# Operands of the dense products at different places modulo 2048 bytes

## The reference, cut to what matters

```python
# first block, each layer
h = rms_norm(x, pre_gain) * (1.0 + scale) + shift
proj = h @ w_in                       # then attention, retention, gated linear attention
y = jnp.concatenate([a_out, r_out, g_out], axis=-1) @ w_out
x = x + gate * rms_norm(y, post_gain)

# second block, each layer: mixers (window attention, spatial gating, fourier), then
def squared_relu_mlp(h, w1, w2):      # w1 is 1024 x 4096, w2 4096 x 1024
    return jnp.square(jax.nn.relu(h @ w1)) @ w2
```

## Time and profile before

| | |
|---|---|
| median of 3 runs | 3961.57 us |
| profiled execution, its own time | 3959.07 us |
| its span | 3957.3 us |
| mean granted TensorE clock | 0.976 of full speed |
| TensorE busy, matmul | 3674.5 us (93% of the span) |
| VectorE, ScalarE, GpSimd busy | 2127.4, 1725.4, 1775.3 us |
| DMA, mean | 106 GB/s |

### The profile page before, as it was taken

The page is one execution under the profiler, slowest core; times in us unless marked ns, Lnnn a source line. Parts: engine busy times, 40 slices in busy tenths (PEclk is TensorE's granted clock), DMA queues, the critical chain, the costliest instruction groups (busy, mean ns, idle before and its releaser), DMA issues.

```text
span 3957.3 us, 61376 instructions
## 1 busy us (share of the span) xinstructions
PE 3674.5 (93%) x22388; PEld 2983.7 (75%) x22388; DVE 2127.4 (54%) x3355; ACT 1725.4 (44%) x2899; POOL 1775.3 (45%) x1288
## 2 busy tenths in 40 slices
PE   4999999999997899888999999999899899999997
PEld 3867767777776777667888998887777778888886
DVE  5546556556456567667224655336567674335234
ACT  2355355355354544555324453335454553243233
POOL 1543444344443422325445885555322355455454
PEclk8999999999999999999999999999999999999999
DMA  6433433433433321112232453222221122233323
GB/s 251 132 127 123 150 120 129 136 134 134 132 111 109 111 74 52 56 59 88 95 99 95 150 170 108 96 96 82 97 70 54 64 80 96 90 96 97 97 94 104
DMA packets 127221, 421.32 MB, mean 106 GB/s; under 512 B 17280, under 2 KB 19104, under 8 KB 126368
## 3 DMA queue, kind: packets, MB, share of 16 engines
q1 hardware_dynamic: 121488, 410.09, 31.2%
q10 hardware_dynamic: 5520, 8.34, 0.6%
HBM read 397.40 MB, written 6.29 MB: 102 GB/s over the span
## 4 chain that ended last, share of the span: by engine, by line
PE 54%; DVE 8%; ACT 3%; issue 2%; POOL 0%; DMA 0%; SPq 0%; ACTq 0%; DVEq 0%; POOLq 0%
PE lin L2673 30%; PE lin L2682 15%; PE bankO L2798 2%; PE lin L2931 2%; PE bankT L2740 2%; DVE x L2318 1%; DVE tmp L2284 1%; DVE y L2317 1%; DVE staged L2296 1%; PE scores L2773 1%; DVE h_lo L2307 1%; ACT whi L1903 1%; PE lin L2815 1%; PE scores L2774 0%; PE lin L2703 0%
## 5 line engine op out<-in xcount | busy, mean ns | idle before, releaser
L1884 POOL TENSOR_TENSOR wlo<-late_raw,whi 128x512 fp32r<-128x512 f32 x456 | 641.5, 1431 | 750.6 <-PE lin L2682 489.8
L1884 POOL TENSOR_TENSOR wlo<-wraw,whi 128x512 fp32r<-128x512 f32 x452 | 635.1, 1428 | 703.5 <-PE lin L2682 485.8
L2673 PE MATMUL lin<-h_hi,whi 128*128 128x512 f32 (+1 forms) x1896 | 709.3, 381 | 48.1 <-ACT y_context L2197 13.8
L2673 PE MATMUL lin<-h_lo,whi 128*128 128x512 f32 (+1 forms) x1896 | 695.9, 374 | 0.0
L525 POOL TENSOR_TENSOR wlo<-wraw,whi 128x512 fp32r<-128x512 f32 x260 | 356.7, 1393 | 465.9 <-PE lin L1170 284.6
L2673 PE MATMUL lin<-a_hi,whi 128*128 128x512 f32 (+1 forms) x1280 | 465.7, 371 | 10.9 <-ACT tmp L2206 8.1
L2673 PEld LDWEIGHTS lin<-h_hi,whi 128*128 128x128 f32 x1896 | 364.2, 192 | 132.3 <-issue 24.3
L2673 PE MATMUL lin<-a_lo,whi 128*128 128x512 f32 (+1 forms) x1280 | 462.6, 369 | 0.0
L1903 ACT ACTIVATE whi<-late_raw 128x1024 fp32r<-128x1024 f32 x228 | 239.2, 1058 | 509.0 <-PE lin L2673 406.8
L1903 ACT ACTIVATE whi<-wraw 128x1024 fp32r<-128x1024 f32 x226 | 237.3, 1058 | 487.1 <-PE lin L2673 402.9
L2682 PE MATMUL lin<-h_hi,wlo 128*128 128x512 f32 (+1 forms) x1896 | 440.4, 375 | 1.2 <-POOL wlo L1884 0.8
(11 more groups left out here) (382 smaller groups left out, 6429.8 us busy)
## 6 DMA issues: line engine op xcount, KB each, us to landing
wraw<-in_w SPq DMA_DIRECT2D x332, 512.0 KB, 3.5
late_raw<-in_w SPq DMA_DIRECT2D x212, 512.0 KB, 3.4
mod_ring<-in_w_ada SPq DMA_DIRECT2D x96, 512.0 KB, 4.5
mod_ring<-in_w_mod SPq DMA_DIRECT2D x32, 512.0 KB, 4.6
tmp<-tmp SPq DMA_DIRECT2D x224, 64.0 KB, 2.0
first_ring<-in_w_mod SPq DMA_DIRECT2D x16, 512.0 KB, 16.6
wraw<-in_dft_tokens SPq DMA_DIRECT2D x16, 512.0 KB, 3.5
late_raw<-in_dft_tokens SPq DMA_DIRECT2D x16, 512.0 KB, 3.5
```

The source lines that it names most:

```text
L1884: last = nc.gpsimd.tensor_tensor(wlo[:, s, half], raw_chunk[r][:, half], whi[:, s, half].bitcast(F32), ALU.subtract)
L2673: last = nc.tensor.matmul(bank[s][:, 0:p.w], whi[:, s, k * P:(k + 1) * P], h[:, k, 0:p.w], start=(k == 0 and h is parts[0]), stop=False)
```

## The change

Only the calls that take SBUF tensors change: their order, and small unused tensors between them. The instructions of every engine, their order, waits and sizes are those of before, and so are all DMAs; only addresses differ.

```diff
-ROW_PAD = 896
...
         staged = sb("staged", [P, KB, W])
+        vc, ms = sb("vc", [P, CTX // P, P]), sb("ms", [P, 16])
         with ExitStack() as mixers:
...
-        a_hi, a_lo = sb("a_hi", [P, FF_CH, W], F32R), sb("a_lo", [P, FF_CH, W], F32R)
+        a_hi = sb("a_hi", [P, FF_CH, W], F32R)
+        sb("pad_inner", [P, P])
+        a_lo = sb("a_lo", [P, FF_CH, W], F32R)
...
-        vx, vc = sb("vx", [P, SEQ // P + 2, P]), sb("vc", [P, CTX // P, P])
+        vx = sb("vx", [P, SEQ // P + 2, P])
...
-        ms = sb("ms", [P, 16])
...
-        t = {"ident": sb("ident", [P, P]), "ones": sb("ones", [P, P]),
-             "cols2": sb("cols2", [P, DEPTH, 2, 2 * 24]), "cols1": sb("cols1", [P, DEPTH, NCOL1]),
-             "mods": sb("mods", [P, MODS, VEC]), "gains2": sb("gains2", [P, DEPTH, 4, KB])}
-        sb("row_pad", [P, ROW_PAD // 4])
-        for name, shape, dt in (("x", [P, KB, SEQ], F32), ("wraw", [P, 2, D], F32), ("whi", [P, 2, D], F32R), ("wlo", [P, 2, D], F32R),
-                                ("h_hi", [P, KB, W], F32R), ("h_lo", [P, KB, W], F32R), ("y", [P, KB, W], F32),
-                                ("tmp", [P, 8, W], F32), ("rstd", [P, W], F32)):
+        t = {}
+        for name, shape, dt in (("ident", [P, P], F32), ("cols1", [P, DEPTH, NCOL1], F32), ("pad_front", [P, 16], F32),
+                                ("whi", [P, 2, D], F32R), ("pad_low", [P, 16], F32), ("wlo", [P, 2, D], F32R),
+                                ("h_hi", [P, KB, W], F32R), ("pad_rows", [P, 48], F32), ("h_lo", [P, KB, W], F32R),
+                                ("ones", [P, P], F32), ("cols2", [P, DEPTH, 2, 2 * 24], F32), ("mods", [P, MODS, VEC], F32),
+                                ("gains2", [P, DEPTH, 4, KB], F32), ("x", [P, KB, SEQ], F32), ("wraw", [P, 2, D], F32),
+                                ("y", [P, KB, W], F32), ("tmp", [P, 8, W], F32), ("rstd", [P, W], F32)):
             t[name] = sb(name, shape, dt)
```

## The result

The changed kernel takes **3991.64 us** in the median of 3 runs (3987.01 to 3995.82), against 3961.57 us before: ratio 1.0078, 95% interval 1.0055 to 1.0101. It is slower by 0.8%. The prediction was 3922 us, faster; the time lies inside the range of 3845 to 3995, on the other side of no change.

A forecast was written before the change was run, and what follows sets the result against it. TensorE's start-to-start product pitch was taken to bound the kernel. Gains of 31.9 us (512 columns) and 14.4 us (256), times 0.85, made 39 us off 3959.1, so 3920 profiled and 3922 us median, range 3845 to 3995 us.

The forecast's parts named there:

- What bounds the kernel: Whole kernel: TensorE bounds it, a product running for 93% of the span, no other engine above 54%.
- the forecast's check list: Feed-forward pitches expected after: a with whi 226.7, a_hi with wlo about 221, h rows about 221 with whi, 226.7 with wlo.
- Step 1: Products of 512 columns whose weights-to-rows distance changes modulo 512: 6016 gain 5.3 ns each, 31.9 us.
- The lower bound of 216: Lowest pitch allowed for 512 columns at new distances, in ns, taken from plain float32 products of 256 columns in two passes.
- The upper bound named there: Highest pitch allowed for 512 columns at new distances: 229.3 ns from ga_both, or 230 after small products.
- the `ga_both` rows: Float32r products with a 32-column weight whose place moves 128 bytes per block; 14 starts average 229.3 ns, never settling.
- The modulus: Distances between rows and weights counted modulo 512, so multiples of 512 count as no change.
- step 2: Products of 256 columns: 2400 gain 6 ns each, half way from 120 to 108, 14.4 us.
- step 3: Share of the products' gain lying on the path: 0.85 in all, 46.3 us becoming 39 us.
- step 4: Other engines' operands moving from 0 to 1472: priced at 0, bounded at 3 us either way.
- The third rival: Pitch no longer settles when distances alternate: products cost about 230 instead of 226.7 ns, 3984 to 4000 us; chance 0.23.
- The two ports: TensorE reads operands through independent ports, so relative place changes nothing; supports the no-difference rival, 3962 us, chance 0.24.

The follow-up runs named there:

- h224_a352: Against the kernel of experiment 1: h rows at 224, inner rows at 352, weights at 0; 4003.55 us beside 3962.55.
- h192_a32: Against the kernel of experiment 1: h rows at 192, inner rows at 32, weights at 0; 4002.12 us beside 3958.96.
- h96_a160: Against the kernel of experiment 1: h rows at 96, inner rows at 160, weights at 0; 4003.81 us beside 3962.55.
- h16_a240: Against the kernel of experiment 1: h rows at 16, inner rows at 240 (modulo 256), tensors used from a 4-element offset; 3994.33 us beside 3964.22.
- experiment 1: Against the changed kernel: dense operands back at 0, the other engines' operands kept at 1472; 3958.97 us, ratio 1.0000.
- only_wlo_64: Against the kernel of experiment 1: wlo alone moved to 64, whi and all rows at 0; 3981.40 us, ratio 1.0055.

## Why the prediction was wrong, point by point

- **What bounds the kernel** held: the other engines are busy as before, the chain has the same shares, and the loss lies in TensorE's pitches.
- **That the pitch hangs on the distance of weights and rows** held, and both parts of it are now shown: places of other engines 1.0000, a common shift 0.9999, and either half of the change 1.005. Of the forecast's check list, `a` with `whi` at 226.7 came out once settled (229.0 and 227.9 with the tails), and `a_hi` with `wlo` is 233.2 where 221 was forecast.
- **The value at other distances is the step that failed.** Step 1 took "half way from 226.7 to 216, a gain of 5.3 ns", 31.9 us less in all. The products of 512 columns cost 33.2 us more, and the runs show losses of 2.2 to 7.6 ns at all nine other distances tried. The argument for the gain was that streams which start together collide, and streams that start apart don't. It has the sign wrong: distance 0 is the best of the ten places. The lower bound of 216 came from products of another kind, whose pitch is firm (in 12 of the 16 pairs of records of L1279 the second starts 216 to 217 ns after the first; a pair is one product of the source, not two as the earlier trace rows was read), but the float32r products of 512 columns came near it in no kernel. The upper bound named there, 229.3 from the `ga_both` rows or 230, was the better witness, and the `ga_both` rows were passed over because their weights are narrow and keep moving. They were the only float32r rows with another distance. A row of the right kind with a flaw should have weighed more than half way to a row of another kind. Even that bound was too low: constant distances reach 234.3.
- **The sign of a distance.** Step 1 calls `a_hi` with `wlo` 64, like `h_hi` with `whi`. Rows less weights it is 512 - 64 = 448, which is 192 modulo 256, and the curve has 233.3 there and 229.0 at 64. The measured 233.2 is that of 192.
- **The modulus.** Step 1 counted in 512. The period is 256, so `h_lo` at 256 did not change its distance to `whi`. Those products still lost most, 12.5 us, for they stand between `h_hi` products at distance 64. The step counted 6016 products as changed. In fact every kind of product of 512 columns in the first table pays: `a_hi` with `wlo` for a distance of its own, the h rows with `whi` for distance 64 in turn with 0, and the products at distance 0 behind a change for the tail.
- **256 columns** (step 2) was right in sign and too large: forecast 14.4 us less, 4.4 us measured in the pitches.
- **The path** (step 3) was about right. The changed kernel alone would say 27.9 us of span for 28.8 us of pitches, 0.97. But in h224_a352, where the time at the 0.50 clock is that of before to 1.1 us, 49.6 us of pitches made 44.5 us of span, 0.90, and in h192_a32, h96_a160 and h16_a240 it is 43.1 of 46.9, 44.7 of 55.9 and 35.3 of 41.3: 0.80 to 0.92, beside the 0.85 taken. These are the four kernels with the largest losses, each in one execution; for the smaller losses the clock moves the spans too much to tell.
- **The other engines** (step 4), priced at 0: confirmed by experiment 1 (1.0000, 0.9990 to 1.0009).
- **The third rival** is what happened: "every product costs about 230 instead of 226.7", 3984 to 4000 us. The measured means are 227.9 to 233.4, and the time 3991.64. It got a chance of 0.23. Its number was better than its reason: it put the loss down to changes of distance alone, while h192_a32, at constant distances, pays 233.3.
- **The two ports.** The rule in the Trainium skill (page "TensorE: Matmul & The Clock Gate", section "Step-by-step: what each phase is for": loading the next tile's weights takes no SBUF read bandwidth from the running matmul) was taken by the prediction to mean that the place of one operand against the other changes nothing. In these traces it does: a shift of one operand against the other moves the settled pitch from 226.7 to as much as 234.3 ns, and a shift of both by 64 moves nothing. Whether the weight load takes read bandwidth, or the two streams hinder each other in another way, no run here shows.

What stays open: why distance 0 still costs 226.7 and not 216 ns, why the curve has its second low at 64, and what sets the order of the values between. The runs show the curve and its period (five places and their fellows 256 bytes on), not the circuit behind it. Only steps of 32, and 16 and 240, were tried, a common shift only by 64, and only with a stationary part of 128 columns; whether a layout with another width of weight would settle elsewhere is open as well.

## What to carry to other kernels

With float32r products of 512 columns at the full clock, put weights and moving rows at the same place modulo 256 bytes, and let all parts that are used in turn have the same distance; at the nine other distances tried here the pitch was 1.0 to 3.4% longer. To price a layout, measure the distance of starts in a long undisturbed row of products, at one distance per kind of row, before mixing several, and compare spans at the same mean clock. Before making products shorter, look for the engine that is hidden by a few hundredths of a microsecond: here GpSimd's 2.86 us under a chunk of 2.88.

## What the runs showed of the hardware that was not expected

- The pitch of float32r products depends on the distance of the two operand streams in SBUF, with a period of 256 bytes: 226.7 ns at 0, 228.9 to 229.0 at 64, 231.7 to 234.3 at the other eight tried. A shift of both by 64 bytes changes nothing (226.7 ns, ratio 0.9999).
- Two distances in turn cost more than either (`h_lo` with `whi`: 229.6 at 64, 228.1 at 0, 233.6 alternating), and after a change of distance the first products of the next kind still pay: in only_wlo_64 231.7 ns over six, then 227.0 over ten.
- For products of 256 columns distance 0 is not the best: h rows of the context take 119.8 ns at 0, 117.2 at 64, 116.3 at 192, and up to 120.7 at 96.
